# Projection tiles taken through one half of the tokens and then the other, each half copied out by itself

## The reference

```
for l in range(2):                                   # first block
    h = rms_norm(x) * (1 + scale_a) + shift_a
    p = h @ w_in[l]                                  # split into q, k, v, gates, m_q, m_kv, m_kpe
    gla_out = gated linear attention of 4 heads, chunk by chunk, * silu(g_o)
    mla_out = causal attention of 4 heads, q and k from low-rank m_q, m_kv
    x = x + gate_a * (concat(gla_out, mla_out) @ w_out[l])
    h = rms_norm(x) * (1 + scale_f) + shift_f
    x = x + gate_f * (relu(h @ w_mlp_up[l])**2 @ w_mlp_down[l])
p = (layer_norm(x) * (1 + scale) + shift) @ w_in_2 + b_in_2   # second block
... dilated window attention over p's q, k, v (3 dilations), a long convolution, merge, output
```

## Time and profile before

| | us |
|---|---|
| median of 3 runs | 4472.72 (4471.67 to 4480.26) |
| the profiled execution | 4482.78, its span 4480.4 |
| PE busy | 4151.5 (93%) |
| DVE, ACT, POOL busy | 2207.9 (49%), 1431.7 (32%), 131.0 (3%) |
| chain that ended last | PE 83%, DVE 10%, ACT 3%, issue 2% |

### The profile page before, as it was taken

How to read it: one execution, slowest core, us unless ns; L and a number is a source line. 1 busy time by engine, 2 the same in 40 slices (tenths; PEclk the granted TensorE clock), 3 DMA queues, 4 the chain that set the end, 5 groups by cost and what they waited for, 6 DMA issues and landing times.

```text
span 4480.4 us, 47017 instructions
## 1 busy us (share of the span) xinstructions
PE 4151.5 (93%) x18808; PEld 3130.9 (70%) x18808; DVE 2207.9 (49%) x3332; ACT 1431.7 (32%) x2333; POOL 131.0 (3%) x166
## 2 busy tenths in 40 slices
PE   6888889899999988889989999969999999999995
PEld 3566555688888866655668888857777777887774
DVE  6686455543443355445553333343364453546655
ACT  2333435321121233235431221223343343224422
POOL 1100000000000000000000000000000000000001
PEclk9999999999999999999999999989999999999997
DMA  5432300033332120110022222111111111125531
GB/s 185 168 113 77 114 15 10 29 94 94 94 99 71 48 71 24 62 45 1 29 61 71 71 71 66 47 66 52 43 38 48 43 43 62 45 71 206 182 128 46
DMA packets 93665, 325.11 MB, mean 73 GB/s; under 512 B 10376, under 2 KB 11176, under 8 KB 92362
## 3 DMA queue, kind: packets, MB, share of 16 engines
q1 hardware_dynamic: 74874, 250.28, 17.0%
q0 software_dynamic: 18576, 71.84, 5.1%
HBM read 287.47 MB, written 34.60 MB: 72 GB/s over the span
## 4 chain that ended last, share of the span: by engine, by line
PE 83%; DVE 10%; ACT 3%; issue 2%; DMA 0%; POOL 0%; SPq 0%; DVEq 0%; ACTq 0%
PE PS L975 56%; PE PS L1849 4%; PE PS L758 2%; PE PS L2878 2%; PE PS L2664 1%; PE PS L1323 1%; PE PS L1721 1%; PE PS L2291 1%; PE PS L1576 1%; PE PS L1720 1%; PE PS L1570 1%; PE PS L2318 1%; PE PS L2304 1%; PE PS L1750 1%; PE PS L681 1%
## 5 line engine op out<-in xcount | busy, mean ns | idle before, releaser
L975 PE MATMUL PS<-hi,WH 128*128 128x512 f32 x2816 | 1161.7, 413 | 80.8 <-issue 35.5
L975 PE MATMUL PS<-hi,WL 128*128 128x512 f32 x2816 | 1118.7, 397 | 0.0
L975 PE MATMUL PS<-lo,WH 128*128 128x512 f32 x2816 | 1112.8, 395 | 0.0
L975 PEld LDWEIGHTS PS<-hi,WH 128*128 128x128 f32 x2816 | 537.8, 191 | 240.0 <-issue 114.7
L975 PEld LDWEIGHTS PS<-hi,WL 128*128 128x128 f32 x2816 | 537.1, 191 | 123.0
L975 PEld LDWEIGHTS PS<-lo,WH 128*128 128x128 f32 x2816 | 538.1, 191 | 115.9 <-issue 6.5
L515 ACT ACTIVATE WH<-raw 128x1024 fp32r<-128x1024 f32 x304 | 319.9, 1052 | 738.6 <-PE PS L975 588.8
L525 DVE TENSOR_TENSOR WL<-raw,WH 128x1024 fp32r<-128x1024 f32 x264 | 322.9, 1223 | 191.0 <-ACT WH L515 190.6
L975 PE MATMUL PS<-ah,WH 128*128 128x512 f32 x1024 | 403.5, 394 | 0.0
L975 PE MATMUL PS<-ah,WL 128*128 128x512 f32 x1024 | 401.4, 392 | 0.0
L975 PE MATMUL PS<-al,WH 128*128 128x512 f32 x1024 | 397.3, 388 | 0.0
(11 more groups left out here) (423 smaller groups left out, 5374.9 us busy)
## 6 DMA issues: line engine op xcount, KB each, us to landing
adab<-in_w_ada POOLq DMA_DIRECT2D x120, 512.0 KB, 4.6
raw<-in_win SPq DMA_DIRECT2D x104, 512.0 KB, 3.6
raw<-in_up SPq DMA_DIRECT2D x64, 512.0 KB, 3.6
raw<-in_down SPq DMA_DIRECT2D x64, 512.0 KB, 3.6
raw<-in_dft SPq DMA_DIRECT2D x24, 512.0 KB, 3.9
sp_x<-X SPq DMA_DIRECT2D x24, 512.0 KB, 5.4
X<-sp_x SPq DMA_DIRECT2D x24, 512.0 KB, 5.7
raw<-in_wout SPq DMA_DIRECT2D x24, 512.0 KB, 3.7
```

Of the source, the lines that this page charges most:

```text
L975: mm = pe.matmul(bank[b + hf], w[:, k, :], r[:, k, HALF[hf]], start=k == 0 and w is wh and r is hi, stop=k == 7 and w is wl)
```

## The change

Tiles 2 to 15 of the input projections, tiles 1 to 7 of each part of the output projections and tiles 2 to 51 of the second projection now go through all parts of the inner size for half 0, and then for half 1. The number of matmuls and weight loads is the same. Due times: a step is now three matmuls instead of six, half as long; the copies and sums of half 0 get a due time in the middle of the tile (`win_end`, `wout_end`, `project_end`), those of half 1 stay. The steps of the input projection's tiles from 3 on are stretched from 2.0 to 2.1 us per part, those of the second projection from 1.45 to 1.7.

```diff
-def win_end(l, i):
-    return win_at(l, 0) + 18.4 if i == 0 else win_at(l, i + 1)
+def win_end(l, i, hf):
+    if i == 0:
+        return win_at(l, 0) + 18.4
+    return win_at(l, i + 1) if hf or i == 1 else (win_at(l, i) + win_at(l, i + 1)) / 2
...
+def wout_end(l, part, n, hf):
+    return wout_at(l, part, n + 1) - (2.8 if n and not hf else 0)
...
+def project_end(p, hf):
+    if p == 0:
+        return project_at(0) + 18.8
+    return project_at(p + 1) if hf or p == 1 else project_at(p) + BUSY_TILE / 2 + 0.3
...
+        def gemm_by_halves_pe(pe, j, at, hi, lo, b, free, step=1.4):
+            wh, wl = weight_tile(j)
+            for hf in range(2):
+                for k in range(8):
+                    yield at + step / 2 * (8 * hf + k)
+                    if k == 0:
+                        if hf == 0:
+                            pe.wait_ge(*W_LO[j])
+                        free(hf)
+                    for w, r in ((wh, hi), (wh, lo), (wl, hi)):
+                        mm = pe.matmul(bank[b + hf], w[:, k, :], r[:, k, HALF[hf]],
+                                       start=k == 0 and w is wh and r is hi, stop=k == 7 and w is wl)
+                mm.then_inc(*W_MM.next(*((j,) if hf else (j, "first half"))))
...
-            at = first_tile(win_at(l, 0)) if i == 0 else second_tile(win_at(l, 0)) if i == 1 else win_at(l, i)
-            yield from gemm_pe(pe, TILE_OF["win", l, n][0], at, hi, lo, win_bank(i), first if i < 2 else None, free,
-                               1.4 if i < 3 else 2.0)
+            j = TILE_OF["win", l, n][0]
+            if i < 2:
+                at = second_tile(win_at(l, 0)) if i else first_tile(win_at(l, 0))
+                yield from gemm_pe(pe, j, at, hi, lo, win_bank(i), first, free)
+            else:
+                yield from gemm_by_halves_pe(pe, j, win_at(l, i), hi, lo, win_bank(i), free, 1.4 if i < 3 else 2.1)
...
-                    yield win_end(l, i) + 0.1 + 0.2 * hf
+                    yield win_end(l, i, hf) + 0.1 + 0.2 * hf
...
-                    for k in range(4):
-                        yield wout_at(l, part, n) + 1.4 * k
...
+                    order = [(k, hf) for k in range(4) for hf in range(2)] if n == 0 else \
+                            [(k, hf) for hf in range(2) for k in range(4)]
+                    for x, (k, hf) in enumerate(order):
+                        yield wout_at(l, part, n) + 0.7 * x
...
-                    yield wout_at(l, part, n + 1) + 0.2
...
                     for hf in range(2):
+                        yield wout_end(l, part, n, hf) + 0.2
...
-                yield from gemm_pe(pe, TILE_OF["win2", PROJECTED[p]][0], at, m.hi3, m.lo3, project_bank(p),
-                                   first if p < 2 else None, free, 1.45)
+                if p < 2:
+                    yield from gemm_pe(pe, j, second_tile(at) if p else first_tile(at), m.hi3, m.lo3, project_bank(p), first, free)
+                else:
+                    yield from gemm_by_halves_pe(pe, j, project_at(p) + 0.3, m.hi3, m.lo3, 0, free, 1.7)
...
-                    yield (project_at(p + 1) if p else project_at(0) + 18.8) + 0.1 + 0.2 * hf
+                    yield project_end(p, hf) + 0.1 + 0.2 * hf
```

More of the change, by code:

```diff
@@ L1853, in wout_pe @@
+                        for y, (w, lo) in enumerate(((wh, 0), (wh, 1), (wl, 0))):
+                            act_in = wout_low(part, k) if lo else m.woh[:, k, :]
+                            mm = pe.matmul(bank[hf], w[:, n % 2, k, :], act_in[:, HALF[hf]], start=k + y == 0,
+                                           stop=k + y == 5)
+                        if k == 3:
+                            mm.then_inc(*W_MM.next(j, n % 2, hf))
                     W_MM.at[j,] = W_MM.n
@@ L1871, in wout_act @@
                 for hf in range(2):
-                    yield wout_at(l, 1, n + 1) + 0.3 + 0.3 * hf
+                    yield wout_end(l, 1, n, hf) + 0.3 + 0.3 * hf
                     act.wait_ge(*WO_DVE["x", l, 1, n, hf])
```

31 lines of the change are left out of this document (12 added, 19 removed).

## The result

The changed kernel took 4411.56 us (median of 4 runs, 4406.79 to 4418.69), beside 4472.19 us for the kernel before: a ratio of 0.9871, 95% interval 0.9856 to 0.9887, 60.6 us less. Taken once more on another occasion it took 4420.70 against 4472.24 us: 0.9883, 0.9868 to 0.9898, 51.5 us less. It was forecast at 4440, 33 us less, in a range from 4424 to 4463. The direction was right and the gain was one and a half to nearly two times as large as forecast, outside the range both times.

The account below looks back on a forecast made before the run. TensorE, busy 93% of the span, was taken as the bound, so only its idle time, slow clock and matmul order or number count. Gains of 8.4 + 18.2 + 11 + 4 less 6.0, 1.1 and 1.5 gave 33.0 us: 4440, range 4424 to 4463.

Parts of the forecast that it names:

- part 1: Output projection behind the attention: waits for sums vanish at seven boundaries a layer, shorter end; 8.4 us, bounds 6 and 10.
- part 0: Output projection ahead of the attention: early half 0 sums pass norms and rotations; 9.1 us a layer, 18.2 in all.
- the tile after the gated attention: One tile a layer: the 3.22 us copy wait and slow clock behind it go; 5.5 us a layer, 11 in all.
- start of the gated attention, layer 0: The 5.38 us copy wait goes and the chain starts 6.9 us earlier; 4 us stay, bounds 0 and 9.
- rest of the gated attention, with what it costs: No gain at tiles whose gaps the chain sets; costs 6.0 us for interruptions, 1.1 for copies moved into the chain.
- second projection: Only 3.6 us idle, 0.6 of it goes; three transposes waiting for DVE are reached earlier: costs 1.5 us, bounds -4 and +3.6.
- tiles 4 and 9: Gated attention, each layer: removed copy waits return as waits for the chain; 0 us, bounds -6 and +5.
- The price of interruptions: Half-long steps cut tiles up 30 times more, at 0.4 or 0.2 us: 8.8 us, 2.8 hidden, so 6.0 lost.
- (a): Rival: chain waits replace removed gaps in the gated attention, norms are late in part 0; 13 us gained, 4460, chance 0.22.
- (b): Rival: every gain lands near its upper bound, 58 us at the bounds, nearer 50 in practice; 4423, chance 0.08.
- (c): Rival: copies stay behind the same queued work and the wait moves to half 1; only part 1 gains; 4473, chance 0.07.
- (d): Rival: copies moved ahead wait for PE and hold the chain, 50 us lost against 33 gained; 4490, chance 0.05.

Follow-up runs that it names:

- the run with late copies: The changed kernel, but with the copies and sums of half 0 queued at the end of the tile as in the kernel before: 4434.14 us, ratio 0.9923.
- 2.1 and later keys: The kernel before, without halves, with the spacing at 2.1 and the second half's keys due 2.5 us later: 4452.42 us, ratio 0.9962.
- steps of six: The changed kernel with tiles by halves open to other work only after every six matmuls: 4406.84 us; with keys also due 2.5 us later, 4403.86 us.

## Why the prediction was right in its direction and wrong in its size

Each term of the sum beside the stage that answers to it, in the two profiled executions of the changed kernel (rounded one by one, so they miss the sums by 0.1):

| Term | forecast | first | again |
|---|---|---|---|
| part 1 | 8.4 | 6.9 | 7.0 |
| part 0 | 18.2 | 26.5 | 26.5 |
| the tile after the gated attention | 11 | 12.4 | 10.9 |
| start of the gated attention, layer 0 | 4 | 4.0 | 2.8 |
| rest of the gated attention, with what it costs | 0 - 6.0 - 1.1 | 10.0 | 7.8 |
| last input tile and first output tile | 0 | -4.0 | -2.7 |
| attention | 0 | 6.0 | 3.1 |
| second projection | -1.5 | 3.0 | 3.1 |
| sum | 33.0 | 64.7 | 58.4 |

**Part 1 was right.** Six boundaries a layer gave 0.4 to 0.5 us each, 2.8 together, where seven had been counted at 0.5: the first tile of the part still goes through both halves in turn, and the one behind it starts no sooner (6.05 and 6.06 us). The end gave the forecast's 0.7 us a layer. No wait on the sums over 0.3 us is left.

**Part 0: the mechanism was right and the cap was wrong.** The early sum of half 0 did pass the norms and rotations, as the run with late copies shows by losing it. For tile 3 the forecast stopped at 5.2 us, since the eight matmuls of L1576 need the second of the norms. The first four don't need it, and tiles 2 and 3, between which the wait lay, gained 7.4 us. Tiles 4 and 5 gained 4.8 (forecast 3.9), tile 1 1.1: the small waits, set against late norms, went as well, and DVE's norms, pushed back by the early sums, held up nothing that shows in the stage. 13.3 us a layer, above the upper bound of 12. The error was to take the eight matmuls of one row for one instruction with one wait.

**The tile after the gated attention: the number was right, the cause shared.** 12.4 and 10.9 us where 11 stood. The halves do give it by themselves, 12.5 us at the spacing of 2.0; but the kernel before with the spacing of 2.1 has 8.2 of them too. The right number alone could not have told this.

**The start of the gated attention of layer 0 was right in each step, and its number is not shown**: a chain some 6 us earlier, a wait of 6.7 us where the forecast had some 6, 4.0 us net (2.8 again). But the kernels before with 2.1 and with 2.1 and later keys, whose programs are alike up to here, differ by 3.6 us in this stretch (-0.8 and -4.4) behind the same wait of 5.4 us for the copy: tile 3 took 21.1 us at a granted clock of 0.63 in the one, 16.4 us at 0.91 in the other. A gain of 3 to 4 us here is no more than that scatter. Behind the moved wait the clock was low again: the granted clock was 0.65 from 262.25 to 268.00, as it had been 0.50 for 6.4 us behind the wait of 5.38 us in before. That agrees with what the Trainium skill (TensorE: Matmul & The Clock Gate, Why this matters for your kernels) says of idle gaps between bursts of matmuls. What the prediction had concluded from it, that a gap only moved costs as much as before, held in part: tile 4 took 7.1 us more, after tiles 2 and 3 had given 11.0.

**The rest of the gated attention was wrong, by 15 to 17 us, and this is the main miss** (10.0 and 7.8 us gained, where 0 less 7.1 of cost stood). The step that failed is the list of what the change does, which left out that the due times are spaced 2.1 instead of 2.0 us. An edit that adds and removes nothing looked like no cost; the run with it alone gave 19.9 us, more than any term of the forecast. Its share of this stage is shown from both sides: 0.8 us with the halves and without the spacing, 12.2 with the spacing and without the halves, 10.0 and 7.8 with both. For what the halves alone do here the forecast's 0 was right. The upper bound of +5 for tiles 4 and 9 rested on transposes reached 0.9 us late, while the level matmuls of the whole stage waited 12.8 us in 19 pieces, a line of the waits that I hadn't put into the account at all.

**The price of interruptions, 6.0 us, doesn't show.** 24 were added, not 30 (12, 4 and 8, counted in the traces). In the second projection 8 more came with less busy time. In the gated attention PE waits for the chain anyway; I had taken 2.8 of 8.8 us as hidden. By the medians steps of six were 4.7 to 13.9 us faster than the changed kernel, with a shorter wait for wkv, and 3.0 us slower once that wait was gone.

**The second projection** gave 3.0 us instead of costing 1.5: 2.7 of its 3.6 idle us went, where I had let 0.6 go. The three waits of 1.0 us for DVE fell to 0.3, where the forecast had them grow; with steps of six they went too. Here too the diff changes a spacing, 1.45 to 1.7, that the forecast gave no price, and no run separates it from the halves.

**What wasn't foreseen against the change** is the wait for wkv, 4.3 us a layer. It is the prediction's own rule, ask what is late next, applied everywhere except behind the input projection's last tile, whose end sets off the fetch 13 us earlier, in both layers.

**Rivals.** (a) came true only in part: L1404 waits 2.75 us a layer more (1.4 in the second execution) where over 2 us was named as a sign against the forecast, and L1204 7 us a layer more, as the forecast said it might, and it was outweighed. (b), everything lands, at 4423, was the nearest and had 0.08. (c) holds for part 0 in the run with late copies. (d) shows nowhere: no kernel with early copies was slower. The range failed on the side of gain: it stopped at 4424, 49 us, while its own bounds added up to 58 us or 4415, and the part not seen had no bound at all. Of the first profile's 64.7 us, some 6 in the attention are the clock of that execution and owe the change nothing.

## What to carry to other kernels

Price every hunk of a diff, due times and spacings above all: a number that changes no instruction moved this kernel as much as the rewriting of its input projections, and the two together gained hardly more than either until the fetch behind them was dealt with. Before halving tiles to free a bank sooner, move the steps by a tenth of a microsecond and look; and where an engine's queue is in order, put the copy's place forward with the halves, since halves alone kept 7 of 27 us where the queue was full and all of it where it was empty. When a stage ends earlier, look at once at the fetch that its end sets off: one due time moved behind the landing gave 10 to 20 us more by the medians, 10 to 14 by the stages.

## What the runs showed of the hardware

**The granted clock isn't a function of the program.** The same kernel with the same two waits of 1.5 and 0.69 us ran the 6 us behind them at 0.50 (1.2 GHz) in one execution and at 1.00 (2.4 GHz) in another; the untouched attention took 198.4 or 201.3 us by that, and 196.2 us in layer 1 of the kernel with only the output projections by halves. Within one execution it is no different. Two pairs of matmuls of the unit norms in after, one in each layer, behind waits of the same length, with the same matmuls and a wait of 1.26 us ahead of them:

```profile
478.69 1.12 PE L1404 MATMUL PS<-X,ones 128*128 128x512 f32 x2 [2.35 <-ACT X L1446]
...
1826.27 2.07 PE L1404 MATMUL PS<-X,ones 128*128 128x512 f32 x2 [2.35 <-ACT X L1446]
```

The longest case is tile 3 of layer 0 in the kernel before: behind the same wait of 5.4 us for the copy it took 21.1 us at a granted clock of 0.63 with the spacing of 2.1, and 16.4 us at 0.91 in the execution that had later keys too, an edit that comes into play only behind this stage.

So a term of low clock behind gaps of such lengths should be given as a span, from nothing to its full size, and a difference of 3 or 4 us in one stage of one profile is no finding until it comes twice.

**Two executions of one program differ by whole stages.** The first 200 us took 201.4 to 214.8 us with the same instructions, and the changed kernel's medians on two occasions lay 9 us apart, each of 4 runs, while those of the kernel before, five times and mostly of 11 or 12 runs, agreed to 1.4. Stages at full clock with hardly a wait agreed to 0.05 us in all kernels that share their code (tiles 1 to 5 of part 0 by halves, with early sums and steps of three: 45.89 to 45.92), and it is these that tell edits apart.
